# Order of the six matmuls of a contraction block: three for one half of the tokens, then three for the other

## What is computed

```python
for l in range(2):
    shift, scale, gate = split(silu(c) @ w_ada[l] + b_ada[l])
    h = rmsnorm(x, g_pre[l]) * (1 + scale) + shift
    proj = h @ w_in[l]                   # 2048 x 5120 in layer 0, 2048 x 8208 in layer 1
    o = attention(proj) if l == 0 else mlstm(proj)
    y = (o * silu(z)) @ w_out[l]         # 2048 x 2048; z is a part of proj
    x = x + gate * rmsnorm(y, g_post[l])
```

## Time and profile before

| | |
|---|---|
| median of 3 runs | 2595.54 us |
| lowest and highest run | 2592.39 and 2596.79 us |
| profiled execution, first to last instruction (span) | 2596.8 us |
| PE busy | 2449.3 us, 94% of the span |
| PEld busy | 2259.8 us, 87% |
| DVE busy | 1213.0 us, 47% |
| ACT busy | 875.6 us, 34% |
| mean granted TensorE clock | 0.951 of full |
| matmuls, and weight loads | 17089 each |
| of them line 746 | 13152 |

### The profile page before, as it was taken

One profiled execution on the slowest core, in us unless ns is written; L12 is line 12 of the kernel. 1 busy time (PEld: TensorE's weight loads), 2 busy tenths in 40 slices (PEclk: granted clock), 3 DMA queues, 4 the chain that ended last, 5 costly groups with the idle time before them and its releaser, 6 DMA issues.

```text
span 2596.8 us, 42451 instructions
## 1 busy us (share of the span) xinstructions
PE 2449.3 (94%) x17089; PEld 2259.8 (87%) x17089; DVE 1213.0 (47%) x1739; ACT 875.6 (34%) x1303; POOL 65.2 (3%) x108
## 2 busy tenths in 40 slices
PE   5979999999999899999699999999999999989996
PEld 4679989889898598888499999999999999988996
DVE  6663453543544645553943343333343434355424
ACT  5732342332432445553431222121212222234322
POOL 1000000000000000000000000000000000000000
PEclk9989999999999599999899989899999999989998
DMA  8863222222121047777254966774649556616731
GB/s 324 306 211 94 76 55 64 71 66 85 50 68 49 1 151 234 238 242 223 76 111 68 83 85 96 68 98 74 98 66 88 95 88 76 96 50 211 247 81 69
DMA packets 346795, 300.84 MB, mean 116 GB/s; under 512 B 9585, under 2 KB 288361, under 8 KB 345497
## 3 DMA queue, kind: packets, MB, share of 16 engines
q1 hardware_dynamic: 336976, 247.88, 44.9%
q0 software_dynamic: 9360, 50.19, 5.3%
q10 hardware_dynamic: 290, 0.27, 0.0%
HBM read 274.81 MB, written 27.56 MB: 116 GB/s over the span
## 4 chain that ended last, share of the span: by engine, by line
PE 82%; DMA 7%; DVE 5%; ACT 3%; issue 2%; DVEq 1%; ACTq 0%; SPq 0%
PE PJ L746 57%; DMA arena<-in_w_ada 3%; PE MX L938 3%; PE MX L864 3%; PE MX L885 3%; DMA raw<-in_w_in_mlstm 3%; PE PJ L711 2%; PE MX L871 2%; PE MX L1060 1%; PE MX L1070 1%; DMA raw<-in_w_in_attn 1%; PE MX L828 1%; PE MX L1022 1%; DVE strips L1788 1%; DMA obuf<-in_w_ada 1%
## 5 line engine op out<-in xcount | busy, mean ns | idle before, releaser
L746 PE MATMUL PJ<-h_hi,w_hi 128*128 128x272 f32 x4384 | 944.3, 297 | 39.0 <-DVE h_lo L1579 24.7
L746 PE MATMUL PJ<-h_hi,w_lo 128*128 128x272 f32 x4384 | 922.1, 292 | 0.0
L746 PE MATMUL PJ<-h_lo,w_hi 128*128 128x272 f32 x4384 | 920.9, 292 | 0.1
L746 PEld LDWEIGHTS PJ<-h_hi,w_hi 128*128 128x128 f32 x4384 | 713.8, 193 | 73.6 <-issue 38.6
L746 PEld LDWEIGHTS PJ<-h_lo,w_hi 128*128 128x128 f32 x4384 | 705.8, 193 | 0.0
L746 PEld LDWEIGHTS PJ<-h_hi,w_lo 128*128 128x128 f32 x4384 | 701.3, 193 | 0.2 <-issue 0.2
L1521 DVE TENSOR_TENSOR w_lo<-raw,w_hi 128x2048 fp32r<-128x2048 f32 x106 | 242.9, 2292 | 406.5 <-ACT w_hi L1159 406.4
L1159 ACT ACTIVATE w_hi<-raw 128x2048 fp32r<-128x2048 f32 x106 | 202.0, 1905 | 42.1 <-DMA raw<-in_w_in_mlstm 34.6
L1788 DVE TENSOR_TENSOR strips<-arena,strips 128x1024 fp32r<-128x1024 f32 x128 | 153.1, 1223 | 82.2 <-ACT strips L1349 80.4
L1349 ACT ACTIVATE strips<-arena 128x1024 fp32r<-128x1024 f32 x128 | 131.4, 1060 | 107.9 <-DMA arena<-in_w_ada 107.5
L938 PE MATMUL MX<-strips,cT 128*128 128x512 f32 x512 | 141.9, 399 | 17.9 <-DVE strips L1788 17.9
(11 more groups left out here) (303 smaller groups left out, 2137.1 us busy)
## 6 DMA issues: line engine op xcount, KB each, us to landing
arena<-in_w_ada SPq DMA_DIRECT2D x128, 512.0 KB, 5.0
raw<-in_w_in_mlstm SPq DMA_DIRECT2D x64, 1024.0 KB, 14.8
raw<-in_w_in_attn SPq DMA_DIRECT2D x40, 1024.0 KB, 5.6
obuf<-in_w_ada SPq DMA_DIRECT2D x32, 1024.0 KB, 7.8
raw<-in_w_out_attn SPq DMA_DIRECT2D x16, 1024.0 KB, 7.8
raw<-in_w_out_mlstm SPq DMA_DIRECT2D x16, 1024.0 KB, 6.5
x_spill<-arena POOLq DMA_DIRECT2D x2, 4352.0 KB, 12.3
arena<-x_spill POOLq DMA_DIRECT2D x2, 4352.0 KB, 17.7
```

The lines of the kernel that those rows point to most:

```text
L746: last = mm(PJ[:, 2 * pair + f, 0:HT], w, h[:, k, HT * f:HT * f + HT], start=(k == 0 and n == 0), stop=(k == KT - 1 and n == 2))
```

## The change

In `block` the loop over the two token halves becomes the outer one and the loop over the three products the inner one. Before, the six matmuls of a contraction block went hi·hi for half 0, hi·hi for half 1, hi·lo for half 0, and so on, and the destination bank changed with each matmul. After, the three products of half 0 come first, then the three of half 1: the bank changes with every third. The number of matmuls, weight loads, waits and signals is the same, and each bank receives the same products in the same order.

```diff
-                    for n, (w, h) in enumerate(((hi, h_hi), (hi, h_lo), (lo, h_hi))):
-                        for f in range(2):
+                    for f in range(2):
+                        for n, (w, h) in enumerate(((hi, h_hi), (hi, h_lo), (lo, h_hi))):
                             last = mm(PJ[:, 2 * pair + f, 0:HT], w, h[:, k, HT * f:HT * f + HT],
                                       start=(k == 0 and n == 0), stop=(k == KT - 1 and n == 2))
```

## The result

The changed kernel takes 2605.27 us, the kernel before 2597.45 us (medians of 20 runs each; the three runs shown earlier are among them). The ratio is 1.003, with a 95% interval of 1.002 to 1.004: slower by 0.3%, where no change was forecast. It lies inside the forecast's range of 2584 to 2610 us.

A forecast was written before the change was run, and what follows sets the result against it. The prediction took PE to bound the kernel, mostly through line 746's dense matmuls. Its terms summed to 8768 x 0 + 0 = 0, so it forecast the median's level, 2595.5 us, with a range of 2584 to 2610 us.

The forecast's parts named there:

- What bounds the kernel: PE, busy 94%, is 82% of the chain; line 746 alone is 57%, at 125.3 to 125.5 ns a matmul.
- the sign that the prediction set itself: Line 746's long stretches: prediction wrong if their rate differs from 125.4 ns by over 0.4 ns, or only the clock changes.
- Counts: Line 746: 13152 matmuls before and after, same weight loads, waits and signals; cost nothing, though 8768 newly stay in their bank.
- ends of blocks: Contraction block heads and ends: banks emptied as late as before, waits of 24.7 and 3.0 us stay; cost zero.
- the sum: Total over line 746's matmuls: 8768 x 0 + 0 = 0, so the forecast is the median's level, 2595.5 us.
- Same bank against other bank: Successive matmuls of line 746: keeping or changing the PSUM bank costs alike, judged from lines 938, 1080 and 1022; 0.
- A: Rival: in line 746 changing the bank has a price; 11 us gained at the bound, 2584.5 us; chance 0.12.
- B: Rival: second and third product of each half start later in a kept bank; likelier +9 to +18 us; chance 0.16.
- Order of operands: Line 746's weight loads: one per matmul in another sequence, 193 ns each, hidden by the 125 ns matmul; cost zero.
- The bounds of -11 and +53 us: Line 746: unexplained rest per matmul read as 1.2 ns for changing banks (gain 11) or 6 ns for staying (loss 53).
- C: Rival: line 746's bank changes keep the clock down; 67 us would be gained, 2529 us; chance 0.02.
- D: Rival: PE takes one column after another whatever line 746's order; time as forecast; chance 0.70 together with the forecast.

The follow-up runs named there:

- e1: Changed kernel's order of reads, but the destination bank alternates with every matmul as in the kernel before: 1.0033 of before, 48.42 us for 384 matmuls.
- e2: Kernel before's order of reads, but the destination bank changes with every third matmul as in the changed kernel: 1.000 of before, 48.10 us for 384 matmuls.
- e3: Changed kernel with h_hi in place of h_lo, so all moving reads are of one activation tile: kept the changed kernel's slow rate.
- e4: Changed kernel with w_hi in place of w_lo, so a block's six weight loads are of one weight block: kept the changed kernel's slow rate.
- e5: Halves and banks alternate as in the kernel before, tiles and weights follow each other as in the changed kernel: rate of before, 1.0009 of before.
- e13: Changed kernel with h_lo read 16 tokens (64 bytes) further on for half 0, 16 back for half 1: 48.10 us for 384 matmuls.
- e9: Changed kernel with each weight block read 16 columns (64 bytes) further on, 16 back for the last block: 48.37 us for 384 matmuls.
- e6: Changed kernel with the second half read from token 256 instead of 272: 48.2 us for 384 matmuls, 121.27 us for 960.
- e7: Kernel before with the second half read from token 256 instead of 272: 48.2 us for 384 matmuls (one stretch 48.35), 121.27 us for 960.
- e11: Changed kernel with both halves read from token 0: 48.2 us for 384 matmuls, 121.27 us for 960.
- e15: Kernel before with two contraction blocks taken together, each product going half 0, half 1 of one block, then of the next: 1.0011 of before.
- e8: Kernel before with 256 instead of 272 columns in contraction blocks 1 to 15: 45.61 us for 384 matmuls, 118.3 ns per 256-column matmul.
- e14: Kernel before with half 1 read from token 240 instead of 272: 47.59 us for 384 matmuls, 123.9 ns each.

## Why the prediction was wrong

**What bounds the kernel** was right, and was what made so small a rate visible: PE carries the chain, line 746 most of it, and 0.8 ns in 125 became 0.3% of the time. One number was misread: the 125.5 ns of the stretch of 960 are not from start to start, which are 125.3 ns there too. By the sign that the prediction set itself, a rate more than 0.4 ns off 125.4, it failed: 126.1 ns.

**Counts, and ends of blocks** were right. Instructions, waits and signals are the same, the waits for h_lo and w_lo kept their 24 and 7 us, and no idle time came up between the products. The idle time at the heads of blocks grew by 3 us, which the sum had at zero.

**Same bank against other bank: 0.** Right in the value, shown by e1 and e2. Rivals A and B both fall as mechanisms.

**Order of operands: zero.** This is the step that failed. I costed the order as a question of weight loads and of which tile is read. Both are free (e3, e4, e5), as I had it. What I left out is where in the row the moving operand begins. The kernel before alternates the starts 0 and 272 tokens, the changed one repeats each three times, and the second costs 0.8 ns a matmul, 10.9 us at most; e13 takes it away again by moving one read in three by 64 bytes.

**Why the rows did not show it.** I took line 938 for "just what the new order does". It stays in one bank and changes the tile with each matmul, but its matmuls are of 512 columns, 32 lines, so that its starts all lie on even lines; it never had an odd start. Its weights also change at every second matmul only. The rows are of plain float32, at half the columns a second, with 1 to 3 ns over; they bear on the bank and not on this. Neither could bound a cost that belongs to float32r with 272 columns. The bounds of -11 and +53 us, and the range up to 2610 us, held it all the same. That was luck: the upper ends were the price of staying in a bank, which e1 and e2 measured as nothing. What was sound in them is that they came from the part of the rate that I could not explain, and that is where I should have stayed: with 12 ns unexplained in each matmul of a line that fills 57% of the span, a chance of 0.72 for less than 0.6 ns of change was too high.

**Rival B** had the sign and a price of the right size (1.2 ns against 1 to 2), by luck. Its place was wrong, since the steps that stay in a bank are no longer than those that change it, and its cause was wrong in both its forms, the sums just written (e1, e2) and the other tile (e3). **C** had no part: the clock is 0.953 after 0.951. **D** was wrong: the order is not free.

**Open:** the exact rule. The starts of the moving reads to 64 bytes change the rate (e13), the starts of the weight reads shift it slightly (e9), and the same instructions can run at one of two rates (e6, e7, e11, e15). This looks like two streams of reads that fall into step in one way or another, but no run measured a conflict, and both simple rules, even and odd by turns and distance modulo four lines, failed in one run or more.

## What to carry to other kernels

Where float32r matmuls follow each other without a gap, the loop order and the cut of the free dimension decide where each read begins, and that alone moved the rate here by up to 1.8% (123.9 to 126.1 ns for 272 columns); the PSUM bank did not. Try a few orders and cuts and compare the lengths of long unbroken stretches with the same count in the profile, which tell 0.1% in one look, before paying for repeated timings; take several stretches of each kernel, since one sequence can have two rates. And when a row is taken as a stand-in for an operation, compare its sizes and starts too, not only its kind, bank and tiles.

## What the runs showed of the hardware

- The destination bank of successive matmuls may change each time or every third time at the same rate, 48.10 us in 384 with the old reads and 48.42 with the new, whichever way the banks go.
- At the 2.4 GHz level a float32r matmul took 125.3 ns for 272 columns in the order of before and 118.3 for 256 (e8), about 0.43 ns a column and 6 to 8 ns fixed, where 113.3 and 106.7 ns are the columns' own. At 1.2 GHz nothing is left over: 226.7 ns from start to start for 272 columns, before and after.
- Reads of the moving operand that differ by 64 bytes in their start change the rate: 48.42 to 48.10 us in 384 (changed kernel and e13), and 48.10 to 47.59 with a second half from token 240 instead of 272 (e14).
- A steady sequence can have two rates at the same granted clock of 1.00: 125.6 and 126.1 ns from start to start in e6, e7 and e11, 125.0 and 125.8 in e15. In e7 the rate changed within a stretch.
- The start of the weight reads changes the pattern of steps and the rate: 48.42 to 48.37 us in 384 (changed kernel and e9).
